# Fourier stage of a two-block layer kernel: folded samples split by the parity of their index

## Chip, cores and metric

One core of one Trainium2 chip. The time is the device time of one execution in microseconds; the median of three runs of the kernel before is 3131.31 us (3128.35 to 3132.95). Everything is float32 outside; inside, most products are made of three passes over fp32r halves.

## What is computed

The kernel computes one hybrid layer (attention, convolution and Fourier branches merged into a residual stream) and then a second block. The change touches only the Fourier branch of the first layer, which works on 512 channels (four groups of 128) of 1024 samples:

```python
def fourier_mix(u):
    b, l, w = u.shape
    ug = u.reshape(b, l, N_FGROUPS, w // N_FGROUPS).astype(jnp.float32)
    y = jnp.fft.fft2(ug, axes=(1, 3), norm='ortho').real
    return y.reshape(b, l, w).astype(u.dtype)

y_f = (fourier_mix(f_u) * silu(f_z)) @ w_br_f
```

`f_u` and `f_z` are two 512-wide slices of `h_lat @ w_in + b_in`. The real part of the two-dimensional transform is cos over time times cos over channels, less sin over time times sin over channels.

## The kernel before

The kernel is a row of stages, each a block with one instruction stream per engine; semaphores join them. Weights come in chunks of 128 x 8 x 128 over the SP queue (`stream`, L277); ScalarE rounds a chunk to `w_hi` in two halves (`round_chunk`, L294), GpSimd forms the rest `w_lo` (`rest_chunk`, L302), and TensorE's `product` (L313) multiplies with three passes per 128 x 512 tile (`w_hi` by `h_hi`, `w_hi` by `h_lo`, `w_lo` by `h_hi`; the call is L323). A full chunk is 48 such matmuls. A slot of `w_hi` is free again when the `used` count of the chunk two back has come.

`fourier` (L1371) loops four times, one group of 128 channels each. The order on TensorE is written out by hand: the product of `f_u` into `ps[0]` (48 matmuls); half of the product of `f_z` into `ps[1]` (24); nine transposes that bring the folded samples to the partitions (L1491, L1492); a quarter of the product of `f_z` (12); the transform over time (L1497 to L1503); the last quarter of `f_z` (12), which covers the eviction of that transform; the product with the 128 x 128 channel tables (L1509 to L1511). `ps` are four two-bank PSUM tensors.

The fold: samples 1 to 511 plus and minus their mirror images 1023 to 513 give `even` and `odd` (VectorE, L1454 to L1456). Sample 512 goes into `mid`. With `cos_t` and `sin_t` of 512 samples by 513 frequencies, the transform over time is four tiles of 128 samples by 512 frequencies for the cosine, the same four by the single frequency 512, four by 512 for the sine, and `mid` by the row `alt` of alternating signs. These operands are plain f32, and each f32 matmul shows as two passes in the trace. The negative frequencies come from symmetry at the end: `y[k] = A[k] - B[k]`, `y[1024-k] = A[k] + B[k]` (L1463 to L1465).

The other engines in one turn of the loop: ScalarE evicts `ps[0]` to `f` (L1426), the transposes to `parts` (L1430), the cosine product to `zc` (L1433, L1434), `silu` of the gate to `z` (L1437, behind a table load), the channel cosine product to `big_a` (L1441, L1442) and rounds the result to `y_hi_t` (L1444). VectorE folds, copies `mid` (L1458) and `zs` (L1460), unfolds to `y` (L1463 to L1465) and multiplies with `z` (L1468). GpSimd forms `y_lo_t` (L1415), behind which stand, on its queue, the rests of the next chunk (L307). `y` shares its buffer with `f`. The constant tables are loaded by SP at the start of the stage (L1401 to L1404), ahead of the weight chunks.

The stage behind is the third `merge`. Its SP stream first waits for the last `y_lo_t` (`ended["y"]`), then loads the 4 MB input `x` to `res` (L3690), and only then its own weight chunks.

Of the kernel before, what the change touches and what calls it, by code (L numbers as in the profile page):

```python
# [11 lines left out]
P = 128  # L12
T = 1024
# [3 lines left out]
HALF = 512  # L17
CTX = 256
# [23 lines left out]
ACT = mybir.ActivationFunctionType  # L42
ALU = mybir.AluOpType
# [21 lines left out]
def constants():  # L65

    t = np.arange(HALF)[:, None].astype(np.float64)
    k = np.arange(HALF + 1)[None, :]
# [19 lines left out]
    for tile, ws in enumerate(((2, 4), (8, 16))):  # L88
# [7 lines left out]
        "k_alt": (((-1.0) ** k) * norm).astype(f),  # L96
# [53 lines left out]
def first_then_second_block(nc, a, out):  # L150
    ctx = ExitStack()
    with ctx:
# [1218 lines left out]
        def fourier(y_hi_t, y_lo_t, following):  # L1371
# [8 lines left out]
            with ExitStack() as sc:  # L1380
                cos_t = sb(sc, "cos_t", [P, HT, HALF + 1])
                sin_t = sb(sc, "sin_t", [P, HT, HALF + 1])
                alt = sb(sc, "alt", [1, HALF + 1])
# [7 lines left out]
                zc = sb(sc, "zc", [P, HALF + 1])  # L1391
                zs = sb(sc, "zs", [P, HALF])
                big_a = sb(sc, "big_a", [P, HALF + 1])
                z = sb(sc, "z", [P, T])

                gates, terms, added = ended["gates"], ended["terms"], ended["sums"]

                @block.sync
                def _(sp):
                    sp.wait_ge(*added)  # L1400
                    sp.dma_start(cos_t[:], a["k_cos"].rearrange("(t p) k -> p t k", p=P)).then_inc(side_loaded.sem, 16)  # L1401
                    sp.dma_start(sin_t[:], a["k_sin"].rearrange("(t p) k -> p t k", p=P)).then_inc(side_loaded.sem, 16)
# [16 lines left out]
                def _(act):  # L1419
                    with act.Fori(0, N) as i:  # L1420
# [11 lines left out]
                        act.wait_ge(scores.sem, scores.at(1, i, 2))  # L1432
                        act.activation(zc[:, 0:HALF], ps[2][:, 0:HALF], ACT.Copy)  # L1433
                        act.activation(zc[:, HALF:HALF + 1], ps[3][:, HALF:HALF + 1], ACT.Copy).then_inc(exped.sem, 1)  # L1434
# [5 lines left out]
                        act.wait_ge(scores.sem, scores.at(2, i, 2))  # L1440
                        act.activation(big_a[:, 0:HALF], ps[2][:, 0:HALF], ACT.Copy)  # L1441
                        act.activation(big_a[:, HALF:HALF + 1], ps[3][:, HALF:HALF + 1], ACT.Copy).then_inc(exped.sem, 1)  # L1442
# [5 lines left out]
                def _(dve):  # L1448
                    dve.wait_ge(aux.sem, aux.at(1))
                    with dve.Fori(0, N) as i:  # L1450
                        dve_steps.open(i, 3)
# [7 lines left out]
                        dve.wait_ge(scores.sem, scores.at(1, i, 2))  # L1459
                        dve.tensor_copy(zs[:], ps[2][:, HALF:2 * HALF]).then_inc(biased.sem, 1)  # L1460
                        dve.wait_ge(exped.sem, exped.at(2, i, 2))
                        back = y[:, T - 1:HALF:-1]
                        dve.tensor_tensor(y[:, 0:HALF], big_a[:, 0:HALF], ps[2][:, HALF:2 * HALF], ALU.subtract)  # L1463
                        dve_steps.done(dve.tensor_tensor(back, big_a[:, 1:HALF], ps[2][:, HALF + 1:2 * HALF], ALU.add))
                        dve_steps.done(dve.tensor_copy(y[:, HALF:HALF + 1], big_a[:, HALF:HALF + 1]))  # L1465
# [7 lines left out]
                def _(pe):  # L1473
                    with pe.Fori(0, N) as i:
# [14 lines left out]
                        for n, src in enumerate((even, odd)):  # L1489
                            for t in range(HT):  # L1490
                                pe.transpose(ps[2][:, (n * HT + t) * P:(n * HT + t + 1) * P], src[:, t * P:t * P + P], ident[:])  # L1491
# [13 lines left out]
                        product(pe, (1, i, 2), wide(ps[1]), part=(3, 4)).then_inc(used.sem, 1)  # L1505
# [9 lines left out]
            for s, n in ((aux, 1), (aux2, N), (aux3, N), (evicted, N), (evicted2, N), (transposed, N), (tr_evicted, N),  # L1515
                         (scores, 2 * N), (exped, 2 * N), (biased, N), (h_ready, N), (y_hi, N), (y_ready, N)):
                s.passed(n)
# [2242 lines left out]
```

## Time and profile before

| | |
|---|---|
| median of three runs | 3131.31 us (3128.35 to 3132.95) |
| profiled execution | 3133.73 us, its span 3131.9 us |
| granted TensorE clock, mean over the span | 0.975 |
| TensorE busy | 2969.2 us (95%) |
| VectorE, ScalarE, GpSimd busy | 1346.4, 956.3, 1016.9 us |
| the Fourier stage's four turns | about 863 to 1001 us of the span |

A matmul's recorded duration includes the drain of its pipeline, so its cost in a stream is read from the distance of starts, or from the length of a piece of the chain divided by its count; it is not its duration.

### The profile page before, as it was taken

The page shows a single profiled execution, that of the slowest core. Times are in us where ns is not written, and L with a number is a line of the kernel's source. Part 1 is how long each engine was busy: PE and PEld are TensorE (multiplying, and loading weights), DVE is VectorE, ACT ScalarE, POOL GpSimd, SP SyncE. Part 2 cuts the span into 40 slices and gives each one's busy share as a digit, 9 for nine tenths or more (in the row PEclk, how much of TensorE's full clock was granted, in tenths as well). Part 3 has the DMA queues.
Part 4 walks back from the last instruction along what each step waited for, and adds up shares of the span by engine and source line. Part 5 has one row for each costly group of instructions (what it writes and reads, how often), then busy time and mean ns, then how long its engine had stood idle before and what let it go on. Part 6 is the DMA issues. An engine that isn't in the chain of part 4 may idle for free.

```text
span 3131.9 us, 40980 instructions
## 1 busy us (share of the span) xinstructions
PE 2969.2 (95%) x15675; PEld 2378.4 (76%) x15675; DVE 1346.4 (43%) x2181; ACT 956.3 (31%) x1574; POOL 1016.9 (32%) x802
## 2 busy tenths in 40 slices
PE   5999989999999899999999999989977999999998
PEld 3788768888877778787777888757766888888886
DVE  5344430111011024543388999860573423323325
ACT  4444532222222235332354212262332111111113
POOL 3534322323422345322221333303454322323223
PEclk8999999999999999999999999999988999999999
DMA  5211021111121223111111111102221111111111
GB/s 204 53 34 38 11 84 54 47 47 47 47 62 53 72 67 121 46 35 38 46 30 33 44 50 49 40 1 102 68 64 34 47 47 47 47 47 47 54 47 74
DMA packets 261468, 170.47 MB, mean 54 GB/s; under 512 B 23604, under 2 KB 249580, under 8 KB 260205
## 3 DMA queue, kind: packets, MB, share of 16 engines
q1 hardware_dynamic: 259997, 163.70, 17.4%
q10 hardware_dynamic: 1360, 5.24, 0.4%
q8 instruction: 75, 1.23, 0.2%
q14 instruction: 36, 0.29, 0.0%
HBM read 160.46 MB, written 8.45 MB: 54 GB/s over the span
## 4 chain that ended last, share of the span: by engine, by line
PE 82%; issue 7%; DVE 5%; POOL 2%; ACT 2%; DMA 1%; SPq 1%; DVEq 0%; POOLq 0%; ACTq 0%
PE ps L323 66%; PE ps L3598 3%; PE ps L3597 2%; PE ps L3599 2%; DVE score L3016 1%; PE ps L980 1%; PE ps L994 1%; POOL w_lo L307 1%; DVE ssq L1918 1%; DVE h_lo L1908 1%; PE ps L1499 1%; PE ps L1502 1%; PE ps L2430 1%; DMA rows<-in_norm_ffn_post 0%; PE ps L966 0%
## 5 line engine op out<-in xcount | busy, mean ns | idle before, releaser
L323 PE MATMUL ps<-h_hi,w_hi 128*128 128x512 f32 x2864 | 1147.3, 401 | 53.5 <-POOL w_lo L307 24.7
L323 PE MATMUL ps<-h_lo,w_hi 128*128 128x512 f32 x2864 | 1128.9, 394 | 0.0
L323 PE MATMUL ps<-h_hi,w_lo 128*128 128x512 f32 x2864 | 1128.1, 394 | 0.0
L307 POOL TENSOR_TENSOR w_lo<-raw,w_hi 128x512 fp32r<-128x512 f32 (+2 forms) x556 | 657.7, 1204 | 1325.4 <-ACT w_hi L300 1325.2
L323 PEld LDWEIGHTS ps<-h_hi,w_hi 128*128 128x128 f32 x2864 | 545.5, 190 | 179.4 <-issue 40.7
L323 PEld LDWEIGHTS ps<-h_hi,w_lo 128*128 128x128 f32 x2864 | 545.1, 190 | 116.9
L323 PEld LDWEIGHTS ps<-h_lo,w_hi 128*128 128x128 f32 x2864 | 546.0, 191 | 113.3 <-issue 2.9
L300 ACT ACTIVATE w_hi<-raw 128x512 fp32r<-128x512 f32 (+2 forms) x556 | 288.3, 567 | 895.5 <-PE ps L323 683.4
L3547 DVE TENSOR_TENSOR act<-gate,ps 128x1024 f32<-128x1024 f32 x22 | 26.9, 1221 | 446.1 <-PE ps L323 446.1
L3556 DVE TENSOR_TENSOR acc<-acc,ps 128x1024 f32<-128x1024 f32 x160 | 195.4, 1221 | 28.5 <-PE ps L3599 28.5
L1203 DVE TENSOR_TENSOR part<-sig,ps 128x1024 f32<-128x1024 f32 x40 | 48.6, 1215 | 357.2 <-PE ps L323 276.6
L3108 DVE MATCH_REPLACE8 score<-best,score 128x384 f32<-128x384 f32 (+2 forms) x192 | 165.8, 876 | 0.0
L3109 DVE MAX8 best<-score 128x8 f32<-128x384 f32 (+2 forms) x192 | 155.8, 879 | 1.1
L3598 PE MATMUL ps<-w_lo,act_hi 128*128 128x512 f32 x352 | 140.5, 399 | 0.0
L3597 PE MATMUL ps<-w_hi,act_hi 128*128 128x512 f32 x352 | 139.5, 396 | 0.2 <-POOL w_lo L307 0.2
L3599 PE MATMUL ps<-w_hi,act_lo 128*128 128x512 f32 x352 | 138.2, 393 | 0.0
L3487 POOL TENSOR_TENSOR act_lo<-act,act_hi 128x1024 fp32r<-128x1024 f32 x21 | 50.6, 2408 | 187.2 <-ACT act_hi L3518 187.2
L1161 POOL TENSOR_TENSOR acc<-acc,part 128x1024 f32 x40 | 96.9, 2421 | 0.0
L3518 ACT ACTIVATE act_hi<-act 128x1024 fp32r<-128x1024 f32 x22 | 23.3, 1061 | 217.5 <-DVE act L3547 217.5
L3513 ACT ACTIVATE gate<-ps 128x1024 f32<-128x1024 f32 x22 | 22.6, 1027 | 211.2 <-PE ps L323 211.2
L3597 PEld LDWEIGHTS ps<-w_hi,act_hi 128*128 128x128 f32 x352 | 66.1, 188 | 17.1 <-POOL w_lo L307 0.6
L3599 PEld LDWEIGHTS ps<-w_hi,act_lo 128*128 128x128 f32 x352 | 66.1, 188 | 15.7
(427 smaller groups left out, 3434.6 us busy)
## 6 DMA issues: line engine op xcount, KB each, us to landing
raw<-in_w_in SPq DMA_DIRECT2D x88, 512.0 KB, 4.0
raw<-in_w_ffn_gate_up SPq DMA_DIRECT2D x44, 512.0 KB, 3.8
raw<-in_w_out SPq DMA_DIRECT2D x32, 512.0 KB, 3.8
raw<-in_w_gate SPq DMA_DIRECT2D x32, 512.0 KB, 4.2
raw<-in_w_ffn_down SPq DMA_DIRECT2D x22, 512.0 KB, 3.5
w_ada<-in_w_ada SPq DMA_DIRECT2D x8, 1024.0 KB, 11.0
x_tok<-in_x ACTq DMA_DIRECT2D x4, 1024.0 KB, 14.9
residual_gate<-in_w_ada SPq DMA_DIRECT2D x8, 512.0 KB
```

The lines of the kernel that those rows point to most:

```text
L300: act.activation(w_hi[:, s, cut], raw[:, s, cut], ACT.Copy).then_inc(rounded.sem, 1)
L307: pool.tensor_tensor(w_lo[:, s, cut], raw[:, s, cut], w_hi[:, s, cut].bitcast(F32), ALU.subtract).then_inc(split.sem, 1)
L323: last = pe.matmul(dst, w[:, chunk[0] % 2, k], x(k), start=(k == ks[0] and n == 0), stop=(k == ks[-1] and n == 2))
L1161: pool.tensor_tensor(to, to, part[:], ALU.add).then_inc(o_evicted.sem, 1)
L1203: dve.tensor_tensor(part[:], sig[:, u % 2], ps[2 * (u % 2) + 1][:], ALU.mult)\
L3108: top_steps.done(dve.match_replace(part(b), best[:, j], part(b), TAKEN) if marking else dve.max(best[:, j], part(b)))
L3109: dve.max(best[:, j], part(b)))
L3487: pool.tensor_tensor(act_lo[:, f % 2], act32[:], act_hi[:, f % 2].bitcast(F32), ALU.subtract)\
L3556: dve.tensor_tensor(acc[:, t], acc[:, t], outs[t][:], ALU.add).then_inc(o_evicted.sem, 1)
L3597: pe.matmul(dst[:, c:c + HALF], act_hi[:, f % 2, tokens], w[0], start=first, stop=False)
L3598: pe.matmul(dst[:, c:c + HALF], act_hi[:, f % 2, tokens], w[1], start=False, stop=False)
L3599: last = pe.matmul(dst[:, c:c + HALF], act_lo[:, f % 2, tokens], w[0], start=False, stop=final)
```

## The change

The folded samples are split once more, by the parity of their index. For frequency k and 512 - k the cosines of even samples are equal and those of odd samples are opposite; the sines the other way round. So four products of 256 samples by 257 frequencies (0 to 256), each in its own PSUM bank, take the place of two of 512 by 512; VectorE adds and subtracts pairs of them to get both halves of the frequencies. The channel products are four of 257 columns, and the unfolding has four pieces.

```diff
-    t = np.arange(HALF)[:, None].astype(np.float64)
-    k = np.arange(HALF + 1)[None, :]
+    t = (2 * np.arange(QUART)[None, :, None] + np.arange(2)[:, None, None]).astype(np.float64)
+    k = np.arange(QUART + 1)
...
+                K = QUART + 1
+                cos_t = sb(sc, "cos_t", [P, HT, K])
+                sin_t = sb(sc, "sin_t", [P, HT, K])
...
+                zc = sb(sc, "zc", [P, 2, K])
+                zs = sb(sc, "zs", [P, 2, K])
+                big_a = sb(sc, "big_a", [P, 2, K])
+                def bank(n):
+                    return ps[2 + n // 2][:, n % 2 * HALF:n % 2 * HALF + K]
...
# ScalarE
-                        act.wait_ge(scores.sem, scores.at(1, i, 2))
-                        act.activation(zc[:, 0:HALF], ps[2][:, 0:HALF], ACT.Copy)
-                        act.activation(zc[:, HALF:HALF + 1], ps[3][:, HALF:HALF + 1], ACT.Copy).then_inc(exped.sem, 1)
+                        act.wait_ge(scores.sem, scores.at(1, i, 4))
+                        act.activation(cos_even[:], bank(0), ACT.Copy).then_inc(exped.sem, 1)
+                        act.wait_ge(scores.sem, scores.at(2, i, 4))
+                        act.activation(sin_odd[:], bank(3), ACT.Copy).then_inc(exped.sem, 1)
...
-                        act.wait_ge(scores.sem, scores.at(2, i, 2))
-                        act.activation(big_a[:, 0:HALF], ps[2][:, 0:HALF], ACT.Copy)
-                        act.activation(big_a[:, HALF:HALF + 1], ps[3][:, HALF:HALF + 1], ACT.Copy).then_inc(exped.sem, 1)
+                        act.wait_ge(scores.sem, scores.at(3, i, 4))
+                        for n in range(2):
+                            act.activation(big_a[:, n], bank(n), ACT.Copy).then_inc(exped.sem, 1)
# VectorE
-                        dve.wait_ge(scores.sem, scores.at(1, i, 2))
-                        dve.tensor_copy(zs[:], ps[2][:, HALF:2 * HALF]).then_inc(biased.sem, 1)
-                        dve.wait_ge(exped.sem, exped.at(2, i, 2))
-                        back = y[:, T - 1:HALF:-1]
-                        dve.tensor_tensor(y[:, 0:HALF], big_a[:, 0:HALF], ps[2][:, HALF:2 * HALF], ALU.subtract)
-                        dve_steps.done(dve.tensor_tensor(back, big_a[:, 1:HALF], ps[2][:, HALF + 1:2 * HALF], ALU.add))
-                        dve_steps.done(dve.tensor_copy(y[:, HALF:HALF + 1], big_a[:, HALF:HALF + 1]))
+                        dve.wait_ge(exped.sem, exped.at(1, i, 4))
+                        dve.tensor_tensor(zc[:, 0], cos_even[:], bank(1), ALU.add)
+                        dve.tensor_tensor(zc[:, 1], cos_even[:], bank(1), ALU.subtract).then_inc(biased.sem, 1)
+                        dve.wait_ge(exped.sem, exped.at(2, i, 4))
+                        dve.tensor_tensor(zs[:, 0], sin_odd[:], bank(2), ALU.add)
+                        dve.tensor_tensor(zs[:, 1], sin_odd[:], bank(2), ALU.subtract).then_inc(biased.sem, 1)
+                        dve.wait_ge(scores.sem, scores.at(4, i, 4))
+                        dve.wait_ge(exped.sem, exped.at(3, i, 4))
+                        dve.tensor_tensor(y[:, 0:K], big_a[:, 0], bank(2), ALU.subtract)
+                        dve.tensor_tensor(y[:, T - 1:T - 1 - QUART:-1], big_a[:, 0, 1:], bank(2)[:, 1:], ALU.add)
+                        dve.wait_ge(exped.sem, exped.at(4, i, 4))
+                        dve.tensor_tensor(y[:, HALF:QUART:-1], big_a[:, 1, 0:QUART], bank(3)[:, 0:QUART], ALU.subtract)
+                        dve_steps.done(dve.tensor_tensor(y[:, HALF + 1:HALF + QUART], big_a[:, 1, 1:QUART], bank(3)[:, 1:QUART], ALU.add))
# TensorE
+                            by_parity = src[:].rearrange("p (t a) -> p a t", a=2)
                             for t in range(HT):
-                                pe.transpose(ps[2][:, (n * HT + t) * P:(n * HT + t + 1) * P], src[:, t * P:t * P + P], ident[:])
+                                pe.transpose(ps[2][:, (n * HT + t) * P:(n * HT + t + 1) * P], by_parity[:, t // 2, t % 2 * P:t % 2 * P + P], ident[:])
...
-                        for dst, c0, c1 in ((ps[2][:, 0:HALF], 0, HALF), (ps[3][:, HALF:HALF + 1], HALF, HALF + 1)):
-                            for t in range(HT):
-                                pe.matmul(dst, parts[:, t], cos_t[:, t, c0:c1], start=(t == 0), stop=False)
-                            pe.matmul(dst, mid[:], alt[:, c0:c1], start=False, stop=True)
-                        for t in range(HT):
-                            last = pe.matmul(ps[2][:, HALF:2 * HALF], parts[:, HT + t], sin_t[:, t, 0:HALF],
-                                             start=(t == 0), stop=(t == HT - 1))
-                        last.then_inc(scores.sem, 1)
+                        for n, table in ((0, cos_t), (1, cos_t), (2, sin_t), (3, sin_t)):
+                            for t in range(2):
+                                at = n % 2 * 2 + t
+                                last = pe.matmul(bank(n), parts[:, n // 2 * HT + at], table[:, at], start=(t == 0), stop=(t == 1 and n != 0))
+                            if n == 0:
+                                last = pe.matmul(bank(n), mid[:], alt[:], start=False, stop=True)
+                            if n % 2:
+                                last.then_inc(scores.sem, 1)
                         product(pe, (1, i, 2), wide(ps[1]), part=(3, 4)).then_inc(used.sem, 1)
-                        pe.wait_ge(exped.sem, exped.at(1, i, 2))
-                        pe.wait_ge(biased.sem, biased.at(1, i, 1))
-                        pe.matmul(ps[2][:, 0:HALF], chan[:, 0], zc[:, 0:HALF], start=True, stop=True)
-                        pe.matmul(ps[3][:, HALF:HALF + 1], chan[:, 0], zc[:, HALF:HALF + 1], start=True, stop=True)
-                        pe.matmul(ps[2][:, HALF:2 * HALF], chan[:, 1], zs[:], start=True, stop=True).then_inc(scores.sem, 1)
+                        pe.wait_ge(biased.sem, biased.at(1, i, 2))
+                        for n in range(2):
+                            last = pe.matmul(bank(n), chan[:, 0], zc[:, n], start=True, stop=True)
+                        last.then_inc(scores.sem, 1)
+                        pe.wait_ge(biased.sem, biased.at(2, i, 2))
+                        for n in range(2):
+                            last = pe.matmul(bank(2 + n), chan[:, 1], zs[:, n], start=True, stop=True)
+                        last.then_inc(scores.sem, 1)
```

The tables in memory are regrouped to match (parity, sample, frequency), and the counts of the semaphores are adapted.

## Rows read from the trace of the kernel before

**Rows 1.** Page, part 1: busy time, share of the span and instructions.
```profile
PE 2969.2 (95%) x15675; PEld 2378.4 (76%) x15675; DVE 1346.4 (43%) x2181; ACT 956.3 (31%) x1574; POOL 1016.9 (32%) x802
```
**Rows 2.** Chain that ended last, third and fourth turn: start us, length us, what.
```profile
965.57 0.86 PE ps L1509 x2
966.43 0.12 PE ps L1510 x2
966.55 0.96 PE ps L1511 x2
967.51 16.36 PE ps L323 x72
983.87 0.87 PE ps L1491 x8
...
987.61 3.44 PE ps L1499 x8
991.05 1.05 PE ps L1500 x2
992.10 0.98 PE ps L1499 x8
993.08 0.31 PE ps L1500 x2
993.39 3.63 PE ps L1502 x8
997.02 2.75 PE ps L323 x12
```
**Rows 3.** The same chain, first turn.
```profile
883.36 3.44 PE ps L1499 x8
...
889.14 5.33 PE ps L1502 x8
```
**Rows 4.** Stretch of 1 us: PE, PEld, DVE, ACT, POOL busy, granted clock, DMA.
```profile
890.00:891.00 1.00, 1.00 (x3) 0.44 (x2) 0.00 (x0) 0.00 (x0) 0.00 (x0) 0.50 0.00 0
```
**Rows 5.** TensorE in order of time, 256-column passes elsewhere: start us, us.
```profile
73.93 0.28 PE L323 MATMUL ps<-hc_hi,w_hi 128*128 128x256 f32 x1
74.05 0.28 PE L323 MATMUL ps<-hc_lo,w_hi 128*128 128x256 f32 x1
```
**Rows 6.** ScalarE in order of time, third turn's end: start us, us.
```profile
965.76 1.28 ACT L1437 ACT_TABLE_LOAD   x1 [2.22 <-PE ps L323]
967.05 1.11 ACT L1437 ACTIVATE z<-ps,vec 128x1024 f32<-128x1024 f32 x1
968.07 0.59 ACT L1441 ACTIVATE big_a<-ps 128x512 f32<-128x512 f32 x1
```
**Rows 7.** VectorE in order of time, third turn's end and fourth turn.
```profile
968.75 0.69 DVE L1463 TENSOR_TENSOR f<-big_a,ps 128x512 f32<-128x512 f32 x1 [5.18 <-ACT big_a L1442]
969.35 0.68 DVE L1464 TENSOR_TENSOR f<-big_a,ps 128x511 f32<-128x511 f32 x1
...
970.22 1.22 DVE L1468 TENSOR_TENSOR f<-f,z 128x1024 f32<-128x1024 f32 x1
...
982.13 0.14 DVE L1456 COPY even<-f 128x1 f32<-128x1 f32 x1
```
**Rows 8.** Groups by form: 256-wide work that reads PSUM, ScalarE and VectorE.
```profile
L2697 ACT ACTIVATE ym_hi<-ps 128x256 fp32r<-128x256 f32 x8 | 3.0, 379 | 1.0 <-PE ps L2817 1.0
L2746 DVE TENSOR_TENSOR ym_lo<-ps,ym_hi 128x256 fp32r<-128x256 f32 x8 | 3.4, 425 | 4.2 <-ACT ym_hi L2697 4.1
```
**Rows 9.** GpSimd in order of time, fourth turn.
```profile
972.82 2.40 POOL L1415 TENSOR_TENSOR y_lo_t<-f,y_hi_t 128x1024 f32 x1 [23.65 <-ACT y_hi_t L1444]
975.18 2.53 POOL L307 TENSOR_TENSOR w_lo<-raw,w_hi 128x512 fp32r<-128x512 f32 x2
```
**Rows 10.** Waits of the SP queue at the start of the merge behind.
```profile
SPq L3690 <- POOL y_lo_t L1415: 31.3, 1, 31.3
```
**Rows 11.** TensorE in order of time, first merge product behind the stage's last weights.
```profile
1026.45 0.79 PE L323 MATMUL ps<-h_hi,w_hi 128*128 128x512 f32 x1 [8.24 <-POOL w_lo L307]
```

More of the change, by code:

```diff
@@ L17 @@
 HALF = 512
+QUART = 256
 CTX = 256
@@ L95, in constants @@
         "k_sin": (np.sin(angle) * norm).astype(f),
-        "k_alt": (((-1.0) ** k) * norm).astype(f),
+        "k_alt": (((-1.0) ** k[None, :]) * norm).astype(f),
         "k_chan": np.stack([np.cos(2 * np.pi * c / P), np.sin(2 * np.pi * c / P)], 1).astype(f),
@@ L1380, in fourier @@
             with ExitStack() as sc:
-                cos_t = sb(sc, "cos_t", [P, HT, HALF + 1])
-                sin_t = sb(sc, "sin_t", [P, HT, HALF + 1])
-                alt = sb(sc, "alt", [1, HALF + 1])
+                K = QUART + 1
+                cos_t = sb(sc, "cos_t", [P, HT, K])
+                sin_t = sb(sc, "sin_t", [P, HT, K])
+                alt = sb(sc, "alt", [1, K])
                 chan = sb(sc, "chan", [P, 2, P])
@@ L1390, in fourier @@
                 mid = sb(sc, "mid", [1, P])
-                zc = sb(sc, "zc", [P, HALF + 1])
-                zs = sb(sc, "zs", [P, HALF])
-                big_a = sb(sc, "big_a", [P, HALF + 1])
+                cos_even = sb(sc, "cos_even", [P, K])
+                sin_odd = sb(sc, "sin_odd", [P, K])
+                zc = sb(sc, "zc", [P, 2, K])
+                zs = sb(sc, "zs", [P, 2, K])
+                big_a = sb(sc, "big_a", [P, 2, K])
                 z = sb(sc, "z", [P, T])
+                def bank(n):
+                    return ps[2 + n // 2][:, n % 2 * HALF:n % 2 * HALF + K]
                 gates, terms, added = ended["gates"], ended["terms"], ended["sums"]
@@ L1400, in _ @@
                     sp.wait_ge(*added)
-                    sp.dma_start(cos_t[:], a["k_cos"].rearrange("(t p) k -> p t k", p=P)).then_inc(side_loaded.sem, 16)
-                    sp.dma_start(sin_t[:], a["k_sin"].rearrange("(t p) k -> p t k", p=P)).then_inc(side_loaded.sem, 16)
+                    sp.dma_start(cos_t[:], a["k_cos"].rearrange("a (t p) k -> p (a t) k", p=P)).then_inc(side_loaded.sem, 16)
+                    sp.dma_start(sin_t[:], a["k_sin"].rearrange("a (t p) k -> p (a t) k", p=P)).then_inc(side_loaded.sem, 16)
                     sp.dma_start(alt[:], a["k_alt"]).then_inc(side_loaded.sem, 16)
@@ L1450, in _ @@
                     with dve.Fori(0, N) as i:
-                        dve_steps.open(i, 3)
+                        dve_steps.open(i, 2)
                         dve.wait_ge(evicted.sem, evicted.at(1, i, 1))
@@ L1504, in _ @@
-                        last.then_inc(scores.sem, 1)
-                        product(pe, (1, i, 2), wide(ps[1]), part=(3, 4)).then_inc(used.sem, 1)
-                        pe.wait_ge(exped.sem, exped.at(1, i, 2))
-                        pe.wait_ge(biased.sem, biased.at(1, i, 1))
-                        pe.matmul(ps[2][:, 0:HALF], chan[:, 0], zc[:, 0:HALF], start=True, stop=True)
-                        pe.matmul(ps[3][:, HALF:HALF + 1], chan[:, 0], zc[:, HALF:HALF + 1], start=True, stop=True)
@@ new lines, in _ @@
+                        product(pe, (1, i, 2), wide(ps[1]), part=(3, 4)).then_inc(used.sem, 1)
+                        pe.wait_ge(biased.sem, biased.at(1, i, 2))
+                        for n in range(2):
+                            last = pe.matmul(bank(n), chan[:, 0], zc[:, n], start=True, stop=True)
+                        last.then_inc(scores.sem, 1)
+                        pe.wait_ge(biased.sem, biased.at(2, i, 2))
+                        for n in range(2):
+                            last = pe.matmul(bank(2 + n), chan[:, 1], zs[:, n], start=True, stop=True)
@@ L1515, in fourier @@
             for s, n in ((aux, 1), (aux2, N), (aux3, N), (evicted, N), (evicted2, N), (transposed, N), (tr_evicted, N),
-                         (scores, 2 * N), (exped, 2 * N), (biased, N), (h_ready, N), (y_hi, N), (y_ready, N)):
+                         (scores, 4 * N), (exped, 4 * N), (biased, 2 * N), (h_ready, N), (y_hi, N), (y_ready, N)):
                 s.passed(n)
```

## Prediction

> **What bounds the kernel now.** I read first the busy shares: TensorE is busy 95% of the span, and no other engine reaches half of it [rows 1]. Busy time alone does not say that a stage is bound there, so next the chain that ended last, over the Fourier stage. In all four turns it stays on TensorE without a gap: 72 matmuls of L323, transposes, 12 of L323, the transform over time, 12 of L323, the channel product, and straight into the next turn [rows 2]. A turn, from 967.51 to the end of the last quarter (997.02 + 2.75) and the channel product behind it (1.94), is 34.2 us. So what leaves TensorE in a turn comes off the end, as long as nothing else becomes late. The turn's own parts are the prices: the transform over time is 3.44 + 1.05 + 0.98 + 0.31 + 3.63 = 9.41 us, the channel product 0.86 + 0.12 + 0.96 = 1.94 us [rows 2].
>
> **The price of a pass.** An f32 matmul is two passes. Eight passes of 512 columns take 3.44 us, 0.43 us each or 0.84 ns a column; eight of one column still take 0.98 us, 0.12 us each; and eight transposes of 128 columns take 0.87 us, 0.109 us each, or 0.85 ns a column [rows 2]. So a pass costs its columns, with a floor of about 0.12 us, and the floor is not added on top: 128 columns cost no more than one. For 257 columns I take 257 x 0.84 = 0.216 us. Bounds: below, nothing under half of 0.43, which is the same number; above, a fixed part in every pass, the line through 1 column (0.1225) and 512 columns (0.43), which gives 0.277 us. The fp32r passes of 256 columns start 0.12 us apart [rows 5], against 16.36 / 72 = 0.227 us for 512 [rows 2]: half, which speaks for the first.
>
> **Transform over time.** Removed: 9.41 us. Added: four products of two matmuls, 16 passes x 0.216 = 3.46 us. `mid` by `alt` stays, with 257 columns in place of 512; its two passes took 1.05 us where two ordinary ones take 0.86, so 0.19 us is the change to a one-row operand and back, and I keep it: 0.43 + 0.19 = 0.62. The step from f32 back to fp32r is in the 3.63 (3.63 - 3.44 = 0.19) and stays. Sum 4.27 us, saved 9.41 - 4.27 = 5.14 us a turn. The one-column passes (0.98 + 0.31) are the part of this that has nothing to do with halving.
>
> **Channel product.** Columns stay (1025 before, 1028 after), eight passes x 0.216 + 0.10 for the step back = 1.83 us against 1.94: saved 0.11 us.
>
> **Transposes.** As many as before, but the stationary operand is now read with a step of two elements. No row shows such a read. It is bounded by nothing (the load is hidden, as now) and by a doubled pass, 8 x 0.109 = 0.87 us a turn, 3.5 us in all. I take nothing, since a stationary load overlaps the pass ahead of it. The Trainium skill (SBUF — State Buffer, Door 1: The DMA port swizzle, the note on cachelines) says that two hits in a 16-byte line are needed for full rate; a step of two float32 gives exactly two, so by it the price is nothing, on the edge. No row here shows that.
>
> **ScalarE and VectorE between the products.** Before, both evictions started at the end of the sine product; they lie under the 12 matmuls that follow (2.75 us). After, `cos_even` can be evicted when half of the transform is done, 8 passes or 1.7 us before its end. With 0.38 us for a 256-wide eviction and 0.43 for a 256-wide VectorE operation on PSUM [rows 8], `zc` is ready at 0.38 + 2 x 0.43 = 1.24 us after that signal, so 0.5 us before the transform ends. `zs` is ready 1.24 us after its end, some 1.4 with hand-overs, and TensorE asks for it at 2.75 + 0.86 = 3.6 us. Cost nothing; cover left 2.2 us. If that cover is gone, every microsecond late counts four times. Nothing is queued behind those waits that anyone needs earlier: ScalarE's next work is the gate, which waits for the quarter product anyway.
>
> **The chain from the channel product to the next weights.** This one is off TensorE but sets how soon the next turn's second chunk is split. Count from the end of the last quarter, 965.57. ScalarE loads a table and forms `z` until 968.16; `big_a` is evicted behind it from 968.07 on [rows 6]; VectorE starts at 968.75 and reaches the multiplication at 970.22 [rows 7]; `y_lo_t` starts at 972.82, the rests follow at 975.18 and the first half is ready near 976.4 [rows 9]. TensorE asks for it after 48 of the 72 matmuls, at 967.51 + 10.9 = 978.4: cover 2.0 us. After the change VectorE can start behind the first 257-wide `big_a`, some 0.3 us earlier; two 512-wide operations and a copy took 1.47 us to the multiplication, four of 257 take about 4 x 0.34 + 0.1 = 1.45 (0.43 recorded less the 0.09 by which neighbours overlap: 0.69 recorded against 0.60 between starts [rows 7]). So the chain is about 0.2 to 0.3 us shorter, and the turn's start comes 0.11 us earlier: the cover stays near 2 us. The fold is just as before relative to the turn's start: done at 982.3 for transposes at 983.87 [rows 2, 7]. Rounding and rests of the other chunk, and a chunk's load, are as before against the turn's start, in a turn that is 28.9 instead of 34.2 us; GpSimd works under 10 us of it.
>
> **Tables.** Four loads stay four, on the same queue and ahead of the chunks, with half the bytes for the two large ones. Before, the first transform started at 883.36 straight behind the matmuls ahead of it [rows 3], so nothing waited and nothing can be gained. Bounds nothing and nothing.
>
> **The end of the stage.** The next merge's SP queue waits for the last `y_lo_t`, then loads 4 MB, and only then weights [rows 10]; TensorE stands 8.24 us for them [rows 11]. So what counts at the end is when `y_lo_t` is done, not when TensorE leaves the stage. That time moves with the last quarter product plus the shorter chain: four transforms, three channel products, and some 0.2 us.
>
> **The sum.** 4 x 5.14 + 3 x 0.11 + 0.2 = 21.1 us. In the first turn of this execution the sine product took 5.33 us instead of 3.63 [rows 2, 3], with the granted clock at 0.50, the lower level of 1.2 GHz [rows 4], right after the one-column passes; in the other three turns the same passes did nothing to it. So those 1.7 us are a chance, and not in the sum. Against the profiled execution the sum gives 3133.73 - 21.1 = 3112.6, or 3110.9 if that fall is gone too. The median of the runs is 2.4 us below the profiled one, and a fall of the clock may well be the difference; against the median it gives 3131.31 - 21.1 = 3110.2. I take **3110.2 us**.
>
> **Rivals.**
> First, a pass has a fixed part (0.277 us at 257 columns). Then 24 passes a turn cost 1.46 us more and `alt` 0.12: 6.3 us in all, 3116.5. The one-column passes speak for it, the transposes and the 256-column passes against it. 7%.
>
> Second, the transposes with a step of two are slower: 0.87 us a turn, 3113.7 if doubled. Nothing in the profile speaks for or against it. 10%.
>
> Third, a wait takes the place of the work: the chain over ScalarE, VectorE and GpSimd, 2.0 us of cover. If the four reversed or offset unfoldings took 1.22 us each, as a 1024-wide operation does [rows 7], in place of 0.34, it would be 3.5 us longer and lose 1.5 us in each of three turns and 3.5 at the end: 8 us, 3118. Reversed writing was there before at the normal duration, so 4%.
>
> Fourth, the side that ends slower: TensorE's clock. The fall in the first turn shows that this stretch is near what keeps the clock up. Each stretch like that one costs 1.7 us; one in every turn instead of one in four costs 5.1 us more, 3115.3, still faster. It decides only from some 42 us at half clock, a third of the stage's 116 us; with the clock down for 60 us the time would be 3110.2 + 30 = 3140. Against it: the passes that preceded the fall are exactly those removed, and TensorE has no gap here. The Trainium skill (TensorE: Matmul & The Clock Gate, a second failure mode: psum-queue depth-cycling) tells of kernels whose clock goes up and down from short idle spells between groups of matmuls as they cycle through PSUM banks; the change has four banks in place of two and two more waits. By that rule this case would be the likely one; the rows show one fall in four turns. 2% for slower, 4% for the milder form.
>
> That the change does not do what it says: passes times columns in the transform fall from 9226 to 4626 by the code, so only where a third of the saving is eaten by something unseen: 1%, about no change.
>
> **How the numbers follow.** Forecast 72%; first rival 7, second 10, third 4, clock 6, nothing 1. Runs of this kernel spread by 4.6 us, so about 3 us to either side are noise. Low end: 3110.2 - 3.0 - 1.7 for the clock = 3105.5. High end: the first rival's time, 3116.5, which takes in the second and the mild clock form. What a measurement of this kernel tells from no change is about 0.2%, 6.3 us: all but the last cases are beyond it. Faster 0.97, same 0.015, slower 0.015.
>
> **What would show it right or wrong.** The changed profile should have a turn of about 28.9 us; 16 f32 passes of 257 columns at 0.216 us from start to start; transposes still near 0.87 us for eight; no idle time of TensorE ahead of the channel products; `y_lo_t` to the merge's first weights as before, with TensorE's 8.2 us of idle time there still; a granted clock near 1.00 through the stage. It is wrong if passes are over 0.25 us, if waits for `zc` or `zs` show, if L323 waits for GpSimd inside a turn, or if the clock falls in several turns.

## The result, and the profile after

The changed kernel takes 3109.54 us (median of four runs, 3108.17 to 3112.74) against 3132.13 us for the kernel before in the same rounds (3128.35 to 3136.88). The ratio is 0.9928, with a 95% interval of 0.9915 to 0.9940: 22.6 us less. 3110.2 was forecast.

The profiled execution took 3110.34 us, its span 3108.5 us, so it can be set beside the one of before (span 3131.9 us): 23.4 us less. The engines' totals hardly moved but for TensorE:

```profile
PE 2942.4 (95%) x15643; PEld 2370.7 (76%) x15643; DVE 1351.1 (43%) x2197; ACT 956.5 (31%) x1574; POOL 1017.3 (33%) x802
```

TensorE is busy 26.8 us less than in [rows 1], VectorE 4.7 us more. Where the time went is read from the chain that ended last, third and fourth turn (start us, length us, what; the lines of `product` are L324 now, the transposes L1507 and L1508, the transform L1516 and L1518, the channel products L1525 and L1529):

```profile
948.35 0.87 PE ps L1525 x4
949.22 0.87 PE ps L1529 x4
950.09 16.35 PE ps L324 x72
966.44 0.95 PE ps L1507 x8
967.39 0.11 PE ps L1508
967.50 2.73 PE ps L324 x12
970.23 0.87 PE ps L1516 x4
971.10 0.63 PE ps L1518 x2
971.73 2.81 PE ps L1516 x12
974.53 2.75 PE ps L324 x12
```

It stands beside [rows 2]. As before, the chain stays on TensorE from the first transposes to the end of the last quarter product of the fourth turn. The transform is 0.87 + 0.63 + 2.81 = 4.31 us where it was 9.41; the channel product 1.74 where it was 1.94; the transposes 0.95 where they were 0.87. A turn starts 28.91 us after the one ahead, against 34.2. The first turn, from its transposes on:

```profile
879.69 0.94 PE ps L1507 x8
...
884.99 2.81 PE ps L1516 x12
```

It is like the others, where [rows 3] had 5.33 us for the sine passes. The chain from the last quarter product of the third turn (it ends at 948.35) to the weights of the next, on VectorE and GpSimd (start us, us):

```profile
951.25 0.42 DVE L1476 TENSOR_TENSOR f<-big_a,ps 128x257 f32<-128x257 f32 x1 [4.42 <-ACT big_a L1451]
951.59 0.41 DVE L1477 TENSOR_TENSOR f<-big_a,ps 128x256 f32<-128x256 f32 x1
951.92 0.41 DVE L1479 TENSOR_TENSOR f<-big_a,ps 128x256 f32<-128x256 f32 x1
952.26 0.41 DVE L1480 TENSOR_TENSOR f<-big_a,ps 128x255 f32<-128x255 f32 x1
952.79 1.22 DVE L1483 TENSOR_TENSOR f<-f,z 128x1024 f32<-128x1024 f32 x1
```
```profile
957.75 2.53 POOL L308 TENSOR_TENSOR w_lo<-raw,w_hi 128x512 fp32r<-128x512 f32 x2
```

The four unfoldings start 0.33 to 0.34 us apart. VectorE starts 0.28 us sooner behind the quarter product than before, but needs 1.54 us to the multiplication where it was 1.47 [rows 7], so the rests (L308) start 0.21 us sooner, 9.40 us behind the quarter product in place of 9.61 [rows 9]. At the end of the stage, the last `y_lo_t` before and after:

```profile
1007.00 2.39 POOL L1415 TENSOR_TENSOR y_lo_t<-f,y_hi_t 128x1024 f32 x1 [23.65 <-ACT y_hi_t L1444]
```
```profile
984.30 2.40 POOL L1423 TENSOR_TENSOR y_lo_t<-f,y_hi_t 128x1024 f32 x1 [18.39 <-ACT y_hi_t L1453]
```

It starts 7.02 us after the last quarter product ends (984.30 - 977.28), where it was 7.23 us (1007.00 - 999.77). The merge's first two chunks were loaded during the Fourier stage; their 72 matmuls run straight behind the channel product. The first merge product on weights that were queued behind the 4 MB load:

```profile
1003.63 0.79 PE L324 MATMUL ps<-h_hi,w_hi 128*128 128x512 f32 x1 [8.12 <-POOL w_lo L308]
```

As in [rows 11], TensorE stood about 8 us ahead of it. I use one measure below, "the stretch": from the first transposes of the first turn to this matmul. It leaves out what the executions differ in before and behind it. The first transposes of the kernel before:

```profile
879.61 0.88 PE ps L1491 x8
```

So the stretch was 1026.45 - 879.61 = 146.84 us and is 1003.63 - 879.69 = 123.94 us: 22.90 us less. The other 0.5 us of the 23.4 are outside. The piece of it behind the start of the last `y_lo_t` (the load of 4 MB and the weights) differs between the profiles of this document by 0.3 us without a change to it, so differences of the stretch below that are not read.

### The profile page after: what moved, and what is told of

It reads as the page before. It is cut to its first block, busy times and chain, and to the rows that moved or that the text cites. A ratio compares the mean times of both kernels' runs of the same rounds, so it can differ in the third digit from the quotient of the medians.

```text
span 3108.5 us, 40948 instructions
## 1 busy us (share of the span) xinstructions
PE 2942.4 (95%) x15643; PEld 2370.7 (76%) x15643; DVE 1351.1 (43%) x2197; ACT 956.5 (31%) x1574; POOL 1017.3 (33%) x802
## 4 chain that ended last, share of the span: by engine, by line
PE 82%; issue 8%; DVE 6%; POOL 2%; ACT 2%; DMA 1%; SPq 0%; POOLq 0%; DVEq 0%; ACTq 0%
PE ps L324 66%; PE ps L3617 3%; PE ps L3616 2%; PE ps L3618 2%; PE ps L981 1%; PE ps L995 1%; POOL w_lo L308 1%; DVE score L3035 1%; DVE ssq L1937 1%; DVE h_lo L1927 1%; PE ps L2449 1%; DMA rows<-in_norm_ffn_post 0%; PE ps L1516 0%; PE ps L967 0%; DVE h_lo L395 0%
## 5 line engine op out<-in xcount | busy, mean ns | idle before, releaser
L324 PE MATMUL ps<-h_hi,w_hi 128*128 128x512 f32 x2864 | 1142.3, 399 | 54.4 <-POOL w_lo L308 24.4
L324 PE MATMUL ps<-h_lo,w_hi 128*128 128x512 f32 x2864 | 1125.7, 393 | 0.0
L324 PE MATMUL ps<-h_hi,w_lo 128*128 128x512 f32 x2864 | 1124.6, 393 | 0.0
L308 POOL TENSOR_TENSOR w_lo<-raw,w_hi 128x512 fp32r<-128x512 f32 (+2 forms) x556 | 658.2, 1205 | 1324.1 <-ACT w_hi L301 1323.9
L324 PEld LDWEIGHTS ps<-h_hi,w_hi 128*128 128x128 f32 x2864 | 543.9, 190 | 178.5 <-issue 38.8
L324 PEld LDWEIGHTS ps<-h_hi,w_lo 128*128 128x128 f32 x2864 | 543.4, 190 | 117.1
L324 PEld LDWEIGHTS ps<-h_lo,w_hi 128*128 128x128 f32 x2864 | 544.5, 190 | 111.5 <-issue 1.0
L3532 ACT ACTIVATE gate<-ps 128x1024 f32<-128x1024 f32 x22 | 22.6, 1027 | 211.1 <-PE ps L324 211.1
## 6 DMA issues: line engine op xcount, KB each, us to landing
w_ada<-in_w_ada SPq DMA_DIRECT2D x8, 1024.0 KB, 10.9
```

What stands on the lines that cost most here:

```text
L308: pool.tensor_tensor(w_lo[:, s, cut], raw[:, s, cut], w_hi[:, s, cut].bitcast(F32), ALU.subtract).then_inc(split.sem, 1)
L324: last = pe.matmul(dst, w[:, chunk[0] % 2, k], x(k), start=(k == ks[0] and n == 0), stop=(k == ks[-1] and n == 2))
```

## Experiments

Each run of this section, except the two of its last part, is a single profiled execution. The first transposes began between 876.5 and 883.1 us although the kernels are alike up to there, so single times differ by several microseconds for reasons outside the stage, and the stretch just named is compared, not the whole time.

### The step of two in the transposes

```diff
- pe.transpose(..., by_parity[:, t // 2, t % 2 * P:t % 2 * P + P], ident[:])
+ pe.transpose(..., src[:, t * P:t * P + P], ident[:])
```

> The changed kernel, with the transposes reading each 128 samples side by side again instead of every second one; the samples are then grouped by place and not by parity, so the output is another one. Theory A (the step of two is what made the eight transposes 0.95 us instead of 0.87): they fall back to 0.87 us, a turn from 28.91 to 28.83 us, 0.3 us over four turns. Theory B (the 0.08 us come from something else, such as the place of the transposes in the stream): they stay at 0.95 us.

```diff
- by_parity = src[:].rearrange("p (t a) -> p a t", a=2)
- pe.transpose(..., by_parity[:, t // 2, t % 2 * P:t % 2 * P + P], ident[:])
+ by_four = src[:].rearrange("p (t a) -> p a t", a=4)
+ pe.transpose(..., by_four[:, t], ident[:])
```

> The changed kernel, with the transposes reading every fourth sample, so that each 16-byte line of SBUF gives one element of a stationary operand; the output is another one. Theory A (a step costs by the lines it touches, as the Trainium skill's page SBUF — State Buffer says of one hit in a line): well over 0.95 us for the eight transposes, up to a doubled 1.7 to 1.9 us, and a turn up to 0.9 us longer. Theory B (the stationary load is hidden whatever the step): 0.95 us as with a step of two, the turn stays 28.9 us.

The chain, one turn of each: the first row without a step, the second with a step of four.

```profile
905.76 0.87 PE ps L1507 x8
```
```profile
905.89 0.95 PE ps L1507 x8
```

The weight loads of these transposes by themselves (duration ns, least, median and most): without a step, then with a step of four, then the changed kernel with its step of two.

```profile
L1507 PEld LDWEIGHTS ps<-ident,even x16: 137/139/142, 876.5 to 963.5; 128*128 128x128 f32 x16
```
```profile
L1507 PEld LDWEIGHTS ps<-ident,even x16: 198/204/210, 876.6 to 963.9; 128*128 128x128 f32 x16
```
```profile
L1507 PEld LDWEIGHTS ps<-ident,even x16: 194/202/209, 879.3 to 966.5; 128*128 128x128 f32 x16
```

In the first run Theory A holds: the 0.08 us are the step. In the second Theory B's forecast holds, 0.95 us as with a step of two, though a load with a step is not quite hidden. A load with a step takes about 65 ns longer, of which the stream of transposes shows 10 ns each (0.95 / 8 against 0.87 / 8). The rule on cachelines that the prediction took from the Trainium skill (SBUF — State Buffer, Door 1: The DMA port swizzle) is not what these loads do: by its two hits in a line, a step of two float32 is free and one of four is not, and by the same note's count of four float32 that may be strided for free, neither would cost; here both steps cost, and the same.

### How much cover the chain to the weights has

```diff
+ dve.tensor_tensor(scratch[:], y[:], z[:], ALU.mult)      # once; in the next run three times
  dve.tensor_tensor(y[:], y[:], z[:], ALU.mult).then_inc(h_ready.sem, 1)
```

> The changed kernel, with one more 128x1024 product on VectorE (into a scratch tile) ahead of the product that finishes y, so the chain to y_lo_t and to the next weights is 1.15 us longer; the output is the reference's. Theory A (the cover of that chain inside a turn is 2.0 us, and at the end of the stage y_lo_t decides): turns stay 28.91 us, and TensorE's idle time at the start of the merge grows from 8.1 to about 9.3 us. Rival (the cover is used up by the change): turns grow by 1.15 us. Rival (TensorE's own leaving decides at the end): the idle time stays 8.1 us.

> The same with three such products, 3.45 us. Theory A (cover 2.0 us): the turns after the first grow by about 1.5 us, to 30.4 us, with TensorE waiting for GpSimd's w_lo in each; at the end of the stage the idle time grows by about 3.5 us; 8 us in all over the changed kernel. Rival (cover nothing): 3 x 3.45 + 3.45 = 13.8 us. Rival (more cover than counted): only 3.5 us at the end.

With one product more, the turns are 28.91 us and the merge waits longer (TensorE in order of time):

```profile
1002.19 0.79 PE L324 MATMUL ps<-h_hi,w_hi 128*128 128x512 f32 x1 [9.31 <-POOL w_lo L308]
```

From 8.12 to 9.31 us, and the stretch from 877.06 to 1002.19 is 125.13 us, 1.2 longer than in the changed kernel. Theory A holds in both its parts: nothing inside the turns, everything at the end.

With three products the chain that ended last leaves TensorE in each turn:

```profile
884.64 2.75 PE ps L324 x12
...
900.17 1.27 POOL w_lo L308
...
901.57 5.74 PE ps L324 x24
907.30 0.95 PE ps L1510 x8
```

In this kernel the transposes are L1510, and the next ones start at 938.05, so a turn is 30.75 us: 1.84 more than 28.91, not 1.5. The last quarter ends at 887.39, TensorE would want the chunk 1.74 + 10.9 us later, at 900.03, and gets it at 901.57: a wait of 1.5 us, as expected. The other 0.3 us: 24 matmuls behind the wait take 5.74 us where a third of the 16.35 us piece is 5.45. Part of that is only how a wait is read. The profile counts idle time from the recorded end of the matmul ahead, which lasts 0.39 us where the next would have started after 0.23; the first matmul behind the wait then takes 0.33 us to the next start in place of 0.23.

At the merge the same kernel waits 0.94 us for the `w_lo` of its second chunk and 10.47 us at the matmul read above, 2.35 more than 8.12. Theory A had put the whole 3.5 us at the latter. Over the stretch (876.54 to 1009.54, 133.0 us) it is 9.1 us more than the changed kernel, against 8 expected; 3 x 1.84 + 3.5 = 9.0.

### The kernel before, again, and the one-column passes

> The kernel before, unchanged, profiled once more. Theory A (the fall of the granted clock in the first sine product belongs to where the one-column passes happen to fall): it need not recur, and may sit in another turn; the four transforms take 9.41 us each, or one or two of them 1.7 us more. Rival (it belongs to the first turn itself, such as the table load): again 5.3 us in the first sine product and in no other.

```diff
- for dst, c0, c1 in ((ps[2][:, 0:HALF], 0, HALF), (ps[3][:, HALF:HALF + 1], HALF, HALF + 1)):
+ for dst, c0, c1 in ((ps[2][:, 0:HALF], 0, HALF),):
...
- pe.matmul(ps[3][:, HALF:HALF + 1], chan[:, 0], zc[:, HALF:HALF + 1], start=True, stop=True)
...
- act.activation(zc[:, HALF:HALF + 1], ps[3][:, HALF:HALF + 1], ACT.Copy).then_inc(exped.sem, 1)
- act.activation(big_a[:, HALF:HALF + 1], ps[3][:, HALF:HALF + 1], ACT.Copy).then_inc(exped.sem, 1)
```

(the increments move to the evictions ahead; row 512 is then a copy of another frequency's value; the second run has the same kernel)

> The kernel before, without the frequency 512: the one-column passes of the cosine and of the channel product and their evictions are left out (row 512 of the output of the transform holds another value). Theory A (they cost what the chain shows, 0.98 + 0.31 + 0.12 us a turn): a turn is 32.8 us instead of 34.2 us, 5.6 us over four turns, and the granted clock stays at 1.00 through the stage. Rival (TensorE would have hidden part of them): less than 4 us. Of the change's 21 us they are then a quarter, and the halved products are the rest.

> The kernel before without its one-column passes, profiled a second time. Theory A: again 3.64 us for the sine product of all four turns and a granted clock of 1.00. Theory B (chance): 5.33 us in one of them is possible.

The kernel before, profiled once more, does the same in the same place (chain that ended last, first and second turn; then the granted clock, which is the last but two of each row):

```profile
886.88 0.31 PE ps L1500 x2
887.19 5.33 PE ps L1502 x8
...
923.08 3.63 PE ps L1502 x8
```
```profile
887.00:889.00 2.00, 2.00 (x5) 1.08 (x5) 0.00 (x0) 0.00 (x0) 0.00 (x0) 0.62 0.00 0
889.00:891.00 2.00, 2.00 (x3) 0.67 (x2) 0.00 (x0) 0.00 (x0) 0.00 (x0) 0.52 0.00 0
```

So the fall to the lower level of 1.2 GHz came in the first turn in two executions of two, 1.70 us each, and in no other turn. TensorE shows no idle time ahead of it. What did not come is Theory A's move to another turn; the rival's forecast fits. Its example, a table load, does not: the kernel without the one-column passes has the same table loads, and no fall. Without the one-column passes (one of its two executions; the transform is L1497, L1498, L1500 here), the first turn is

```profile
881.24 3.44 PE ps L1497 x8
884.67 1.05 PE ps L1498 x2
885.72 3.64 PE ps L1500 x8
...
892.13 0.86 PE ps L1507 x2
892.99 0.86 PE ps L1508 x2
```

and the other execution has 3.64 us too; both have a granted clock of 1.00 through the stage. The turns are 32.72 us (877.49 to 910.21) in place of 34.2, as expected. The transform loses 1.28 us and the channel product (the last two rows) 0.22, not 0.12: the 0.10 us that the sine part of it had beyond 0.86 go with the one-column passes ahead of it. The stretch is 1016.58 - 877.49 = 139.09 us, and 1019.35 - 879.95 = 139.40 us in the other execution: 7.75 and 7.44 less than before. In both, 7.4 us are gone by the end of the last quarter product, 1.70 of them for the fall.

That is a third of the 22.90 us of the change. Dropping the one-column passes, which has nothing to do with halving, gives some 7.5 us, the 1.70 of the clock among them, and the rest of the change, the halved products above all, the other 15.4.

### The one-column passes put back into the changed kernel

```diff
+                            if n == 1:
+                                for t in range(5):
+                                    pe.matmul(ps[3][:, HALF + 400:HALF + 401], parts[:, t], cos_t[:, 0, 0:1], start=True, stop=True)
```

> The changed kernel, with five one-column matmuls (ten passes) into an unused PSUM column between the cosine and the sine products, where the kernel before had its ten; the output is the reference's. Theory A (those passes bring the fall of the granted clock in the first turn): besides 10 x 0.12 = 1.2 us in every turn, the first turn's sine passes run at the half clock, and what follows them too, 1.5 us or so more, once. Theory B (the fall belongs to the length of the old transform, or to chance): 1.2 us a turn and a granted clock of 1.00 throughout.

```profile
884.13 1.06 PE ps L1516 x4
885.20 1.01 PE ps L1523 x10
886.21 1.85 PE ps L1516 x8
```

The first turn's sine passes (the third row) take 1.85 us, as in the other three turns, and the clock is 1.00 throughout the turns; a turn is 30.04 us, 1.1 more. Theory B holds. In this one execution the passes alone did not bring the fall; in the kernel before it went away without them. The match is not exact: of the ten passes of the kernel before, two had the one-row operand `mid`, and none of these has. Whether the fall needs the one-column passes together with the long 512-column stretch around them, or stood on how the first turn lined up, stays open.

### What a pass costs

```diff
- pe.matmul(bank(n), parts[:, n // 2 * HT + at], table[:, at], start=(t == 0), stop=(t == 1 and n != 0))
+ pe.matmul(bank(n)[:, 0:P + 1], parts[:, n // 2 * HT + at], table[:, at, 0:P + 1], start=(t == 0), stop=(t == 1 and n != 0))
```

(and the same cut for `alt`)

> The changed kernel, with 129 frequencies in place of 257 in the transform over time (the other columns of the banks keep old values, so the output is another one). Theory A (a pass costs 0.84 ns a column, with a floor of 0.12 us that is not added): 16 passes at 0.12 instead of 0.216 us, so 1.5 us less a turn, and alt 0.1 less; a turn is 27.3 us. Rival (a fixed part in each pass, 0.10 us plus 0.45 ns a column, which also gives 0.216 at 257): 16 x 0.16, only 0.9 us less.

```profile
880.78 0.45 PE ps L1516 x4
881.22 0.41 PE ps L1518 x2
881.64 1.54 PE ps L1516 x12
```

A pass of 129 columns costs 0.45 / 4 = 0.113 us; one of 257 cost 0.87 / 4 = 0.217; one of 512 0.43. The transform is 2.40 us and a turn 27.05 us (876.98 to 904.03), where 27.3 was expected. Both theories were too dear: with a fixed part of 0.10 us the pass would be 0.16; with the floor of 0.12 I had taken from one-column passes, 0.12. Columns alone give 129 x 0.84 = 0.108. The line through the passes of 129 and 257 columns leaves a fixed part of 0.01 us, so the rival is out.

### The evictions without cover

```diff
                        product(pe, (1, i, 2), wide(ps[1]), part=(2, 4))
+                        product(pe, (1, i, 2), wide(ps[1]), part=(3, 4)).then_inc(used.sem, 1)
                        pe.wait_ge(side_loaded.sem, side_loaded.at(4))
...
-                        product(pe, (1, i, 2), wide(ps[1]), part=(3, 4)).then_inc(used.sem, 1)
```

> The changed kernel, with the last quarter product of f_z moved ahead of the transform over time, so that nothing covers the evictions between transform and channel product. Theory A (zc is ready before the transform ends, zs 1.2 us after its end, and the first channel product is 0.87 us): TensorE waits about 0.4 us a turn for zs and nothing for zc; the gate is evicted earlier, so the chain to y_lo_t starts 2.3 us earlier against the transform's end, and the end of the stage comes 1.9 us earlier while the turns lose 3 x 0.4: about 0.7 us faster. Rival (the evictions are late, as the prediction's third rival has it): TensorE waits 1.5 us or more a turn and the kernel is 3 us or more slower.

TensorE in order of time, second turn:

```profile
923.30 1.03 PE L1525 MATMUL ps<-zc,chan 128*128 128x257 f32 x4
924.73 1.14 PE L1529 MATMUL ps<-zs,chan 128*128 128x257 f32 x4 [0.40 <-DVE zs L1473]
```

No wait for `zc`, 0.40 us for `zs`: as counted. A turn is 29.59 us (912.65 to 942.24), 0.68 longer: the 0.40 us of the wait and 0.3 us around it, as in the run with three products. But the stretch (883.06 to 1009.23) is 126.2 us, 2.2 longer, where I expected 0.7 shorter. The error is in the expectation: moving the quarter ahead puts the transform later by just the 2.7 us it had covered, so ScalarE cannot start on `z` earlier; it now starts behind the eviction of `sin_odd`, and the end loses 3 x 0.68 and a little more. The order that the kernel has is the better one.

### The load of 4 MB behind the first weights

The 8.1 us in which TensorE stands at the merge end with weights whose loads are queued behind this one; the load itself takes 13.0 us from issue to landing in the changed kernel. There are two merges with such a load, and the edit changes both.

```diff
 # stream(): each turn of the loop ends with
+                if tail:
+                    tail(sp, i)
 # merge(), SP
-                    if early or residual_gate is not None:
-                        sp.wait_ge(*y_done)
-                    if early:
-                        early(sp)
+                    def tail(sp, i):
+                        sp.wait_ge(*y_done)
+                        early(sp, i)
 # load_x, and load_x2 (the other merge) in the same way
-                    sp.dma_start(res[:], a["x"][0].rearrange("(t p) d -> p t d", p=P)).then_inc(x_loaded.sem, 16)
+                    sp.dma_start(res[:, bass.ds(i * 2, 2)], a["x"][0].rearrange("(t p) d -> p t d", p=P)[:, bass.ds(i * 2, 2)]).then_inc(x_loaded.sem, 16)
```

> The changed kernel, with the 4 MB load ahead of each of the two merges that have one cut into four loads of 1 MB, each behind the weight chunks of one turn of the merge's loop, with the wait for the branch's output moved there too. Theory A (TensorE's idle time at the start of those merges is the time that the weights stand behind the 4 MB): the 8.1 us of idle time go, and the stretch at the half clock behind them (some 4 us lost), at both merges: 15 to 25 us faster than the changed kernel, so about 3090 us. Rival (the weights wait for y_lo_t in any case, or the pieces delay later chunks by as much): under 5 us.

> The same, with the last quarter product of f_z ahead of the transform as well. If the end of the stage is no longer set by y_lo_t, that move can only lose its 4 x 0.4 us: the same as the run beside it or 1.6 us slower. If y_lo_t still decides, 0.7 us faster.

The first takes 3091.23 us (3088.39 to 3091.85, four runs), 0.9861 of the kernel before in the same rounds (0.9842 to 0.9880): below the interval of the change alone, and about 18 us under its 3109.54. Two windows of 20 us around the merge's start, first of the changed kernel, then of this one (TensorE busy is the second number, the granted clock the last but two):

```profile
980.00:1000.00 20.00, 15.51 (x68) 12.39 (x66) 2.70 (x6) 3.48 (x6) 3.79 (x3) 0.97 0.63 232
1000.00:1020.00 20.00, 16.37 (x60) 13.27 (x61) 1.22 (x1) 6.59 (x10) 8.15 (x8) 0.77 0.21 58
```
```profile
980.00:1000.00 20.00, 20.00 (x89) 16.39 (x89) 2.77 (x4) 7.36 (x10) 10.30 (x9) 1.00 0.13 40
1000.00:1020.00 20.00, 20.00 (x89) 16.43 (x88) 1.22 (x1) 4.17 (x6) 6.49 (x6) 1.00 0.32 106
```

The idle time is gone and so is the stretch at a granted clock of 0.5 behind it. At the second merge of this kind the changed kernel waited 4.1 us for weights, and this one does not. Of the 18.7 us between the two profiled spans, 1.3 were there before the merge began; the first merge gave 11.0 us (8.1 of idle time and 2.9 behind it, where the slower clock was) and the part with the second merge 6.7 us (4.1 of idle time). Theory A holds.

The second, with the quarter ahead as well, takes 3100.16 us (3095.73 to 3103.54), 0.9896 (0.9877 to 0.9916). That is 9 us over the run beside it, where at most 1.6 had been expected. In the profiles the stage, from the first transposes to the merge's first product, is 2.66 us longer (101.96 against 99.30), about 4 x 0.68 again. The two profiled executions differ by only 3.9 us, and 1.2 of them lie outside the stage. But the profiled execution of the second kernel was the fastest of its four, so most of the rest of the 9 us stands in no trace, and I have no cause for it.

## Why the prediction was right

**The bound.** TensorE carried the stage and still does: from the first transposes to the end of the last quarter product it needs 97.59 us in place of 120.16, 22.57 less, and the stretch lost 22.90. The turn was put at 28.9 us and is 28.91.

**The transform over time.** Predicted 4.27, measured 4.31 us a turn: 5.10 saved, four times 20.4 us. The pass was priced at 0.216 and costs 0.217; the first rival, a fixed part in every pass, falls with the run of 129 columns. The runs without the one-column passes split the term: those passes are 1.28 us of the 5.10, the part that the prediction said has nothing to do with halving. One reading of the prediction was wrong without harm here: the 0.19 us in the last piece is not the step back to fp32r. The channel product steps back too and takes 0.87 us for four passes, with nothing on top. The 0.19 stands on the passes right behind the one-row `alt`: in the run with the passes put back the four behind it take 1.06 us in place of 0.87. `alt` stayed, and so did the 0.19.

**Channel product.** 1.74 instead of 1.83, so 0.20 saved a turn instead of 0.11. The prediction had kept 0.10 us "for the step back" here. Without the one-column pass the old channel product takes 0.86 + 0.86 us, with the same step back behind it, so the 0.10 belonged to the one-column pass and went with it.

**Transposes.** Taken at nothing, with a bound of 0.87 us a turn; they cost 0.08. The second rival was right in kind and a tenth of its price; the reason given for nothing, that the load is hidden, was not quite so.

**The chain and the end of the stage.** The chain was to be 0.2 to 0.3 us shorter and is 0.21 shorter, though the four unfoldings take 1.54 us to the multiplication and not 1.45. `zc` and `zs` came when they were expected to, by the run without cover: no wait for one, 0.40 us for the other. The cover of 2.0 us inside a turn and the whole weight at the end were borne out by the runs with one and three products more: 1.15 us more cost nothing in a turn, 3.4 us more made TensorE wait 1.5 us. What the third rival left out is that a turn with such a wait is longer by 0.3 us more than the idle time that the profile shows.

**The sum, and the term that was off.** 20.4 + 3 x 0.20 - 4 x 0.08 + 0.2 = 20.9 us, beside the 21.1 forecast. The stretch lost 22.90. The difference is the 1.70 us of the clock in the first turn, and 0.3 us are left over. The prediction's step "those 1.7 us are a chance, and not in the sum" did not hold: it made the median of before free of the fall because it lies 2.4 us below the profiled execution. The second profile of the kernel before has the fall and took 3128.74 us, below that median. The fall came in both profiled executions of the kernel before and in none of the twelve of the others. So the 1.7 us belonged into the sum, which would have given 22.8 us against 22.6 measured. That the forecast of 3110.2 came within 0.7 us of 3109.54 is in part luck: the saving was 1.5 us short, and the base 0.8 us below the median of the later rounds, which made up for half of it. Both are small beside the 4.6 us over which the runs of one kernel spread.

**The clock as a rival.** There was no fall in any turn of the changed kernel, nor in those of its nine variants. The rule on cycling through PSUM banks that was set beside it (the Trainium skill, TensorE: Matmul & The Clock Gate, the section on psum-queue depth-cycling) speaks of short idle spells between groups of matmuls. The changed kernel has four banks and two more waits, but TensorE stood for none of them, so it does not test that rule. The runs with 0.40 us and with 1.55 us of idle time in a turn come nearer to it, and their granted clock was 1.00 through the turns as well.

## What to carry to other kernels

When a product on the bounding engine is halved by symmetry, price it by columns streamed, count each odd one-column leftover like a pass of some 128 columns (0.10 to 0.12 us here), and then check two things only: whether the added combining work ends before the engine asks for it, and which event sets the end of the stage. A leftover can weigh more than its passes: here the one-column passes and what went with them were a third of the gain. The end of the stage was set not by the engine's own leaving but by a transfer queued behind the stage's last output. Moving it, and its like at the second block's merge, behind the weights was worth 18 us, nearly as much as the change itself; 11 of them at this stage's end.

## What the hardware did that was not expected

- A stationary load of 128 float32 columns with a step of two or four elements takes 202 to 210 ns against 139 to 143 ns without one, and the same for both steps; in the stream of transposes 10 ns of it show.
- An f32 pass of 129 columns (0.113 us) costs about what one of a single column does (0.123 us in the kernel before, 0.10 us where ten were put into the changed kernel).
- The fall of the granted clock came in the same place of the first turn in both profiles of the kernel before, and in none of the two without its one-column passes; putting ten one-column passes into the changed kernel did not bring it back in one execution.
- A turn in which the profile shows TensorE idle for 0.4 or 1.55 us is longer by some 0.3 us more than that.
